# Mixer A's visits split into half steps, and the first two projection tiles interleaved

## What is computed

```python
h = rmsnorm(x, g_mix); z = h @ w_in            # 44 tiles of 128 columns
# mixer A: 16 heads x 64, ALiBi, three windows (128,1), (512,4), (2048,16), outputs mixed by their softmax denominators
# mixer B: 16 query heads, 4 key heads, window 128, with a learned sink
y = concat(oa * silu(ga), ob * silu(gb)); h = x + y @ w_out
out = h + (p @ w_ple) * sigmoid(rmsnorm(h, g_ple) @ w_pg); final rmsnorm
```

## Time and profile before

| | us |
|---|---|
| median of 3 runs | 2344.28 (2338.28 to 2345.48) |
| the profiled execution | 2341.7 |
| its span | 2339.9 |
| TensorE busy in it | 2278.0 |
| VectorE, ScalarE, POOL busy | 905.0, 565.0, 771.8 |

### The profile page before, as it was taken

How to read it: one execution, slowest core, us unless ns; L and a number is a source line. 1 busy time by engine, 2 the same in 40 slices (tenths; PEclk the granted TensorE clock), 3 DMA queues, 4 the chain that set the end, 5 groups by cost and what they waited for, 6 DMA issues and landing times.

```text
span 2339.9 us, 39175 instructions
## 1 busy us (share of the span) xinstructions
PE 2278.0 (97%) x15570; PEld 2179.3 (93%) x15570; DVE 905.0 (39%) x2334; ACT 565.0 (24%) x1562; POOL 771.8 (33%) x783
## 2 busy tenths in 40 slices
PE   4999999999999999999999999999999999999996
PEld 4999999999999999999988999899999999999996
DVE  7123333333324413455555424343233373222235
ACT  5122222222222212323544310210000030000374
POOL 2232222222222133222222233343333344555564
PEclk9999999999999999999999999999999999999998
DMA  5144454444444425455464454454343555444666
GB/s 196 61 125 96 104 117 96 108 114 96 109 111 96 107 71 147 131 147 146 138 160 142 135 174 131 158 139 111 86 102 92 122 164 133 113 115 109 194 202 224
DMA packets 542140, 299.71 MB, mean 128 GB/s; under 512 B 245140, under 2 KB 507300, under 8 KB 540668
## 3 DMA queue, kind: packets, MB, share of 16 engines
q1 hardware_dynamic: 464277, 254.82, 41.1%
q10 hardware_dynamic: 77680, 42.39, 6.3%
HBM read 230.76 MB, written 66.36 MB: 127 GB/s over the span
## 4 chain that ended last, share of the span: by engine, by line
PE 90%; DVE 4%; DMA 2%; ACT 2%; POOL 1%; issue 0%; SPq 0%; DVEq 0%; ACTq 0%; POOLq 0%
PE psum L1081 26%; PE psum L1083 26%; PE psum L1082 26%; PE psum L889 3%; PE psum L911 2%; PE psum L922 2%; PE psum L951 1%; PE psum L979 1%; PE psum L966 1%; DMA h_stage<-h_scratch 1%; DVE x_n L1554 1%; DVE act_lo L1545 1%; PE psum L986 1%; POOL w_lo L845 0%; DMA x_in<-in_x_prompt 0%; DVE act_lo L1912 0%
## 5 line engine op out<-in xcount | busy, mean ns | idle before, releaser
L1081 PE MATMUL psum<-act_hi,w_hi 128*128 128x344 f32 x4032 | 1303.4, 323 | 6.6 <-POOL w_lo L845 5.3
L1083 PE MATMUL psum<-act_hi,w_lo 128*128 128x344 f32 x4032 | 1286.9, 319 | 0.0
L1082 PE MATMUL psum<-act_lo,w_hi 128*128 128x344 f32 x4032 | 1286.1, 319 | 0.0
L1081 PEld LDWEIGHTS psum<-act_hi,w_hi 128*128 128x128 f32 x4032 | 758.2, 188 | 17.9 <-issue 12.4
L1083 PEld LDWEIGHTS psum<-act_hi,w_lo 128*128 128x128 f32 x4032 | 757.5, 188 | 0.0
L1082 PEld LDWEIGHTS psum<-act_lo,w_hi 128*128 128x128 f32 x4032 | 757.2, 188 | 0.2
L843 POOL CAST w_hi<-w_raw 128x512 fp32r<-128x512 f32 (+1 forms) x352 | 222.8, 633 | 1464.1 <-PE psum L1083 1274.9
L845 POOL TENSOR_TENSOR w_lo<-w_raw,w_hi 128x512 fp32r<-128x512 f32 (+1 forms) x390 | 508.7, 1306 | 59.6 <-ACT w_hi L1488 31.3
L1657 DVE COPY prob_t<-psum 128x512 f32<-128x512 f32 (+1 forms) x56 | 35.5, 634 | 391.5 <-PE psum L922 391.5
L1958 DVE TENSOR_TENSOR t_gate<-psum,acc 128x344 f32<-128x344 f32 x48 | 24.7, 515 | 224.9 <-PE psum L1083 224.9
L1889 DVE TENSOR_TENSOR h_row<-psum,h_row 128x344 f32<-128x344 f32 x48 | 22.1, 513 | 212.9 <-PE psum L1083 212.9
(11 more groups left out here) (208 smaller groups left out, 1787.4 us busy)
## 6 DMA issues: line engine op xcount, KB each, us to landing
w_raw<-in_w_in SPq DMA_DIRECT2D x208, 256.0 KB, 3.0
w_raw<-in_w_pg SPq DMA_DIRECT2D x94, 256.0 KB, 2.8
w_raw<-in_w_out SPq DMA_DIRECT2D x64, 256.0 KB, 2.7
z_scratch<-stage ACTq DMA_DIRECT2D x72, 172.0 KB, 1.9
h_scratch<-h_row ACTq DMA_DIRECT2D x16, 516.0 KB, 2.7
x_in<-in_x_prompt SPq DMA_DIRECT2D x8, 1024.0 KB, 5.1
zq<-z_scratch SPq DMA_DIRECT2D x32, 256.0 KB, 3.9
out<-z_sq SPq DMA_DIRECT2D x128, 64.0 KB, 2.8
```

What stands on the lines that cost most here:

```text
L1081: pe.matmul(psum[:, bank, 0:T3], hi_w, hi_a[:, k, rows], start=(k == 0), stop=False, skip_group_check=True)
L1082: pe.matmul(psum[:, bank, 0:T3], hi_w, lo_a[:, k, rows], start=False, stop=False, skip_group_check=True)
L1083: return pe.matmul(psum[:, bank, 0:T3], lo_w, hi_a[:, k, rows], start=False, stop=stop, skip_group_check=True)
```

## The change

Mixer A gets half steps: 8 in 144 positions, an even one at 36 (s // 2) with the values of chunks already turned and then the scores of one or two chunks, an odd one 22 positions behind it with only turns, of one or two chunks. A pair has 12 half steps, and pair n's last four are shared with the next pair's first four. A chunk has a slot of two banks (2 and 3, or 4 and 5) for scores and turn alike; copies go back in place into `prob`, `prob_t` is gone; the two halves of the output have banks 6 and 7. Where two chunks are scored in a visit, both wait for what the first waits for. VectorE and SP follow, with the low half of the values turned as the first thing of half step 2.

The head: three slots for x, normalised in place; `pick` loaded ahead of `g_row`; three tiles turned before the first unit; the units of the first two weight tiles interleaved (by thirds), with eight groups of weights held; in the very first unit all products with `act_hi` first, then those with `act_lo`; the other tiles turned at positions 12, 17, 26, 39, 44 and 48. The rest is a later load of the sink table and merged semaphores.

```diff
-X_FIRST = 4
-X_LATER = {4: 4, 8: 5, 13: 6, 19: 7, 27: 8}
+X_FIRST = 3
+X_LATER = {12: 3, 17: 4, 26: 5, 39: 6, 44: 7, 48: 8}
+X_BANKS = 24
+LO_AFTER = {1: (0,), 2: (1, 2), 4: (3,), 5: (4, 5), 7: (6,)}
+HEAD_TILES = 2
+HEAD_UNITS = [(i, t) for t in range(3) for i in range(HEAD_TILES)]
+HEAD_BANKS = [0, 1, 6, 7, 0, 1]
+HEAD_GROUPS = 8
...
+def x_place(u):
+
+    return 2 + u % 6 if u < X_BANKS else 2 + (u - X_BANKS) % 4
...
+def x_before(u):
+
+    return u - 5 if u < X_BANKS + 4 else u - 3
...
+def last_unit(tile):
+
+    return 2 * HEAD_TILES + tile if tile < HEAD_TILES else 3 * tile + 2
...
+def freed_before(u):
+
+    if u < 4:
+        return 0
+    return u - 3 if u < len(HEAD_UNITS) else u - 1
...
 NCH = len(A_PARTS)
-SCORE_AT = [0, 2, 3, 4, 5, 6, 8]
-TURN_AT = [7, 4, 5, 6, 8, 9, 10]
-TURN_ORDER = [1, 2, 3, 0, 4, 5, 6]
-SCALE_AT = [6, 3, 4, 5, 6, 7, 9]
-SCALE_ORDER = [1, 2, 3, 4, 0, 5, 6]
-PLACE = [(0, 8, 12, 4, 8, 12, 0), (4, 8, 12, 0, 8, 12, 4)]
-PLACE_FREE = [(-1, 3), (-1, 4), (-1, 5), (-1, 6), (0, 1), (0, 2), (0, 0)]
-A_STEPS = 13
+A_HALVES = 8
+A_STEPS = 12
+SCORE_AT = [0, 2, 2, 4, 4, 6, 8]
+SCORED_WITH = [0, 1, 1, 3, 3, 5, 0]
+TURN_AT = [7, 3, 3, 5, 5, 7, 9]
+TURN_ORDER = [1, 2, 3, 4, 0, 5, 6]
+SCALE_ORDER = [1, 2, 3, 4, 5, 0, 6]
+A_SLOT = [0, 0, 1, 0, 1, 1, 1]
+PLACE = [0, 4, 8, 4, 8, 4, 4]
+PLACE_FREE = [(-1, 0), (-1, 6), (-1, 4), (0, 1), (0, 2), (0, 3), (0, 5)]
 SQUARE_AT = [1, 2, 4, 6]
 NSQ = len(SQUARE_AT)
 V_HIGH, V_LOW, K_HIGH, K_LOW = range(NSQ)
...
+def scored_before_step(n, c):
+
+    if c == NCH - 1:
+        return scored_before(n + 1, A_FAR) if n + 1 < PAIRS else scored_before(n, c)
+    return scored_before(n, SCORED_WITH[c])
...
-    for g in range(7, WG * (NZ - 2) + 7):
-        tile, part = divmod(g - 7, WG)
-        put(16 * (3 * tile + 2) + 4 * (part + 1), "weights", g)
+    for g in range(HEAD_GROUPS + 2, WG * (NZ - 2) + 7):
+        tile, part = divmod(ring_before(g - 2), WG)
+        put(16 * last_unit(tile) + 4 * (part + 1), "weights", g)
...
-        for s in range(NCH if n + 1 < PAIRS else A_STEPS):
-            put(176 + 144 * n + (144 * s // NCH if n + 1 < PAIRS else 14 * s), "a", n, s)
+        for s in range(A_HALVES if n + 1 < PAIRS else A_STEPS):
+            put(176 + 144 * n + (36 * (s // 2) + 22 * (s % 2) if n + 1 < PAIRS else 32 * (s // 2) + 20 * (s % 2)), "a", n, s)
+        put(176 + 144 * n + 50, "a_low", n)
...
-        x_in, x_n, g_row = at(W_END, ("x_in", [P, 2, D], F32), ("x_n", [P, 2, D], F32), ("g_row", [P, D], F32))
+        x_in, x_sq, g_row, w_hi_head, w_lo_head = at(
+            W_END, ("x_in", [P, 3, D], F32), ("x_sq", [P, D], F32), ("g_row", [P, D], F32),
+            ("w_hi_head", [P, HEAD_GROUPS - WRING, WG, P], F32R), ("w_lo_head", [P, HEAD_GROUPS - WRING, WG, P], F32R))
...
             for i, (r0, n) in enumerate(ROW_TILES):
-                if i >= 2:
-                    sp.wait_ge(sem("x_normed"), i - 1)
-                sp.dma_start(x_in[0:n, i % 2, :], x_p[r0:r0 + n, :] if i < 8 else x_s).then_inc(sem(f"x_loaded{i % 2}"), 16)
+                if i >= 3:
+                    sp.wait_ge(sem("x_turned"), 4 * (i - 2))
+                sp.dma_start(x_in[0:n, i % 3, :], x_p[r0:r0 + n, :] if i < 8 else x_s).then_inc(sem(f"x_loaded{i % 3}"), 16)
                 if i == 0:
                     sp.dma_start(ident[:], a["c_ident"]).then_inc(sem("consts"), 16)
+                    sp.dma_start(pick[:], a["c_pick"]).then_inc(sem("consts"), 16)
                     sp.wait_ge(sem("x_loaded0"), 16)
                     sp.dma_start(g_row[:], bcast_rows(a["g_mix"][0:1, :], P)).then_inc(sem("consts"), 16)
-                elif i == 1:
-                    sp.dma_start(pick[:], a["c_pick"]).then_inc(sem("consts"), 16)
...
-                for g in {1: (0, 1), 2: (2,), 3: (3,), 5: (4,)}.get(i, ()):
+                for g in {2: (0, 1), 3: (2, 3), 4: (4, 5), 5: (6, 7)}.get(i, ()):
                     weights(g)
-            for g in range(5, 7):
+            for g in range(HEAD_GROUPS, HEAD_GROUPS + 2):
                 weights(g)
 
...
                     more = n + 1 < PAIRS
                     if s == 1:
                         store_squares(n, V_HIGH)
+                        load_zv(n, 0)
                         sp.wait_ge(sem("fstat_stored"), 16 * (n + 1))
                         sp.dma_start(n_stat[:, n % 2].rearrange("p m h b -> p (m h) b"), fs_dram[n % 2].rearrange("m (b p) -> p m b", p=P),
                                      allow_slow_non_contiguous=True).then_inc(sem("nstat_loaded"), 16)
...
                     elif s == 2:
-                        load_zv(n, 0)
                         load_v_nat(n, 1)
                     elif s == 3:
-                        store_squares(n, V_LOW)
-                    elif s == 4:
                         load_v_nat(n, 0)
...
-                        if more:
-                            load_zv(n + 1, 1)
                         store_squares(n, K_LOW)
                     elif s == 8 and more:
+                        load_zv(n + 1, 1)
+                    elif s == 9 and more:
                         sp.wait_ge(sem("a_biased"), 2 * scored_before(n, NCH - 1) + 2)
                         load_bias(n + 1)
                         sp.wait_ge(sem("a_scored"), 2 * scored_before(n, NCH - 1) + 2)
                         load_zq("a", n + 1, 0)
-                    for half, at_s in ((1, 9), (0, 12)):
+                    for half, at_s in ((1, 9), (0, 11)):
                         if s == at_s:
                             store_o("a", n, half)
...
+                elif e[0] == "a_low":
+                    store_squares(e[1], V_LOW)
...
             def a_scores(n, c):
-                first = scored_before(n, c)
+                first, bank = scored_before_step(n, c), 2 + 2 * A_SLOT[c]
...
-                        if i == 0 and first:
-                            pe.wait_ge(sem("a_biased"), 2 * (first - 1) + h + 1)
-                        mm = pe.matmul(psum[:, 2 + h, col:col + w], queries(half), keys(half), start=True, stop=True)
+                        if i == 0 and h == 0 and first:
+                            pe.wait_ge(sem("a_biased"), 2 * first)
+                        mm = pe.matmul(psum[:, bank + h, col:col + w], queries(half), keys(half), start=True, stop=True)
                         if i == len(pieces) - 1:
                             mm.then_inc(sem("a_scored"), 1)
 
...
                 pe.wait_ge(sem("a_copied0"), before + 1)
                 pe.wait_ge(sem("a_copied1"), before + 1)
...
-                        mm = pe.matmul(psum[HD * h:HD * h + HD, 6, c0:c1:step], values[:, HD * h:HD * h + HD], prob_t[:, h, x * P:(x + 1) * P],
+                        mm = pe.matmul(psum[HD * h:HD * h + HD, bank, c0:c1:step], values[:, HD * h:HD * h + HD], prob_of(c)[:, h, x * P:(x + 1) * P],
                                        start=(c in (1, 4) and x == 0), stop=(c in (A_FAR, NCH - 1) and x == len(pieces) - 1), skip_group_check=True)
                 mm.then_inc(sem("a_summed"), 1)
 
             def a_turns(n, c):
-                before = turned_before(n, c)
+                before, bank = turned_before(n, c), 2 + 2 * A_SLOT[c]
                 pe.wait_ge(sem("a_scaled"), scaled_by(n, c))
                 for h in range(2):
                     if before:
                         pe.wait_ge(sem(f"a_copied{h}"), before)
...
 
             def a_step(n_, s_):
                 for n, s in a_walked(n_, s_):
-                    if s in SCORE_AT:
-                        a_scores(n, SCORE_AT.index(s))
+                    for c in TURN_ORDER:
+                        if TURN_AT[c] == s - 1:
+                            a_values(n, c)
+                for n, c in a_chunks(n_, s_):
+                    a_scores(n, c)
                 for n, s in a_walked(n_, s_):
-                    if s - 1 in TURN_AT:
-                        a_values(n, TURN_AT.index(s - 1))
-                for n, s in a_walked(n_, s_):
-                    if s in TURN_AT:
-                        a_turns(n, TURN_AT.index(s))
+                    for c in TURN_ORDER:
+                        if TURN_AT[c] == s:
+                            a_turns(n, c)
 
             def b_step(n_, s_):
                 g = n_ // 2
...
                 if k % WG == 0:
                     pe.wait_ge(sem("w_split"), GROUP[what, tile, k] + 1)
 
+            def first_unit():
+
+                rows = slice(0, T3)
+                pe.wait_ge(sem("x_hi"), 4 * 3)
+                for k in range(KT):
+                    if k in X_LATER:
+                        x_turn(X_LATER[k])
+                    group_wait("in", 0, k)
+                    hi_w, lo_w = split_place(GROUP["in", 0, k - k % WG], WG)
+                    pe.matmul(psum[:, 0, 0:T3], hi_w[:, k % WG, :], act_hi[:, k, rows], start=(k == 0), stop=False, skip_group_check=True)
```

(54 more changed lines are left out.)

154 lines of the change are left out of this document (93 added, 61 removed).

## The result

The changed kernel takes 2369.24 us (median of four runs, 2366.61 to 2373.76) against 2343.89 us of the kernel before on the same chip: ratio 1.0115, 95% interval 1.009 to 1.0139. It is about 25 us **slower**. I had forecast 2340.8, within 2328 to 2352, so both the forecast and the range missed. The profiled execution is the slowest of the four, 2373.8 us with a span of 2371.9.

A forecast was written before the change was run, and what follows sets the result against it. TensorE, busy 97% of the span, was taken as the bound: only what it does or waits for counts. Mixer A's visits -12.5, copy wait +17 and head -8 gave -3.5 us: 2340.8 by the median, range 2328 to 2352.

The forecast's parts named there:

- Visits, -12.5 us: Mixer A: four visits of values and scores lose 0.55 us each, turns 0.01; -12.5 us over eight pairs (-17 to -4).
- Alone it would have given the wrong sign: Rival for the whole kernel: counting drains only, mixer A only gains, giving the first rival's time, 2323.8; no chance given.
- Wait inside a visit of turns, +17: Mixer A, half steps 3, 5, 7: second chunk waits for the first's copies, 0.71 us 24 times, +17 (+9 to +24).
- The chain between scores and turns: Mixer A: two chunks are biased, exponentiated and scaled within 22 positions, 10.3 us; effect 0.
- Two us spare: 0: Mixer A: chunk 1 ready at 8.1 us (needed 10.3), chunk 2 at 9.4 (needed 11.7), so no cost.
- It eats half a us of the spare: Mixer A: turning the low square ends about 10 us after half step 1 began; chunk 1's scores are out at 9.6.
- 2 us or more to spare: SP's queue: zv, v_nat, bias and zq are issued a few positions earlier or later, each with that margin.
- The second rival: Mixer A: low values load late behind SP's stores, turns start 1.5 us late in each pair; +12, 2352.8; chance 0.17.
- Head, -8: First projections: last row tile turned and TensorE at position 48 at 66.7 us, before 74.8; -8 us (-14 to -3).
- The sum: Whole kernel: -12.5 + 17 - 8 = -3.5 us, 2338.2, by the median 2340.8; no change.

The follow-up runs named there:

- e8: Changed kernel with e5's four edits, and the low half of v_nat loaded by its own event at position 58 (52 in the last pair): 2326.05 us, ratio 0.9921.
- e1: Changed kernel without the wait on the previous chunk's copies inside a_turns: 2359.33 us, ratio 1.007.
- e2: Changed kernel with own buffers for the low half of the values and its square, loaded with the high half: 2348.63 us, ratio 1.0021.
- e3: Changed kernel with the edits of e1 and e2 together: 2337.86 us, ratio 0.9972.
- e4: Changed kernel with every odd half step at position 26 instead of 22, except in the last pair: 2360.91 us, ratio 1.008.
- e5: Changed kernel with e3's edits, the last row tile's turn at position 56, and half step 3 at 26 (24 in the last pair): 2343.88 us, ratio 1.0002.

## Why the prediction was wrong

- **Visits, -12.5 us: right.** In e8, where no visit waits, they sum to 158.1 us (12.3 + 24.6 + 121.2 for all others) against 168.8 before: -10.7. A visit of turns of one chunk costs 0.87 us for a stream of 0.85, so turns are free to enter and leave. A visit of values and scores loses 0.60 us (that of half step 4 costs 3.59 for streams of 2.99, by the prediction's 0.053 us for 128 columns) where I took 0.55. (Visits that score the far chunk lose 1.1 us more, in both kernels.) So the rule of the Trainium skill, "TensorEngine Tiling (Array Packing)", Key Properties, that a change of the tiling mode drains the engine, agrees with these visits (0.60 us lost where the mode changes, 0.02 where it doesn't). Alone it would have given the wrong sign for the kernel.
- **Wait inside a visit of turns, +17: right in mechanism and price.** A visit takes 2.20 us with it and 1.53 without, 16 times, which is 10 to 11 us; in half step 3, the other eight times, a longer wait covered it.
- **The chain between scores and turns, put at 0: this step failed.** The prediction found "Two us spare: 0", and of the low half's load that "It eats half a us of the spare". The working gave 9.0 us from half step 1 to the low half's landing; it was 12.6 in pair 2. Term by term: VectorE's square of the high half was done at 3.1, not 2.3. SP was 2.0 us late for it, since at the same visit it has the previous pair's two biases, zq and output to issue, behind four weight groups; of bias and zq I wrote that they have "2 us or more to spare", and asked when they would be late, not whom they make late. The stores took 3.8 us to issue, not 2.2. The load took 3.6, less than the 4.5 assumed. Behind that the chain itself was 1.7 us longer than in the earlier trace rows (bias to scaled 10.4 us, not 8.7), all of it in the scaling. Some 3.4 us late and 1.7 longer, against 2.2 spare, is a wait of 2.9 us; TensorE's idle time is recorded as 2.58.
- **The second rival had the mechanism, not the size.** It named that wait at +12 us, from one duration (6.5 us for the load) that never occurred: the loads of the low half took 3.3 to 4.5 us in the eight pairs. The lateness came from the queue ahead of the load. And the rival priced idle time only: 16.8 us of waits for the scaling made half step 3 24.6 us dearer, with another 3 us or so of projections at half clock behind them.
- **Head, -8: the mechanism right, the size off.** The changed kernel's profile shows -3.5, the head alone -5.4 by the medians. TensorE reached position 48 at 68.8 us, not 66.7, VectorE being 1.9 late with the last tile (65.85 against 64), and then lost some 2.6 us more to the half clock, for which the sum had no term.
- **The sum.** In the profiled executions mixer A's +33.2 is -10.7 for the clean visits, +10.7 for the copy waits of half steps 5 and 7, and some 33 for half step 3 over its clean 12.3 with the slow projections behind it. Of these 33 about 5 are the hidden copy waits. By the medians the whole change is +25.4, where the two profiled executions are 32.1 apart; how the 6.7 us less are shared out isn't known. e1 and e2 measured the two main losses as 9.9 and 20.6, and some 6 us more are the second chunk's late scaling that e2 and e3 still have and e8 doesn't.

## What to carry to other kernels

When steps are merged, work out for each DMA the time at which its queue comes to it, with everything that now stands ahead at the same visit; a landing time from an unhurried queue doesn't tell when a load is there. Take away all waits of a place together, or expect the next one (the load, then the stores, then the second chunk, then v_nat). And price a stall of TensorE with the half clock that can come behind it: in the head it made 5 us of 2.

## What the runs showed of the hardware

- **Half clock after a short stall, but not after every one.** Idle 2.58 us ahead of the turns brought the granted clock to the lower level for the visit and 3 us more, in pairs 2 and 4 of the changed kernel. The length of the stall doesn't decide alone. In the changed kernel 1.92 us ahead of the turns cost just themselves in pair 1 (4.39 us for the visit) and were followed by 2.7 us of slow projections in pair 6 (5.08). Stalls of 0.59 and 0.74 us (e2, e4) had nothing behind them. In e5 six idle times of 1.0 to 1.95 us ahead of half step 4 cost just themselves (4.66 to 5.60 us for the visit, 3.59 clean), and two of 1.97 and 2.16 us cost 7.25 and 7.45. Two of these by TensorE's timeline, pair 3 and pair 1:

```profile
436.31 1.75 PE L987 MATMUL psum<-prob,v_nat 128*64 128x128 f32 x28 [1.95 <-issue]
255.67 2.10 PE L987 MATMUL psum<-prob,v_nat 128*64 128x128 f32 x28 [1.97 <-issue]
```

- **VectorE stands while GpSimd splits weights.** The row of VectorE at 343.52 above is an instruction on 2 elements in each partition that took 1.14 us, 0.16 elsewhere; the next row takes 2.11 us for two pieces in place of 0.61. GpSimd's timeline of the changed kernel at that time:

```profile
343.35 1.29 POOL L918 TENSOR_TENSOR w_lo<-w_raw,w_hi 128x512 fp32r<-128x512 f32 x1
...
345.27 1.26 POOL L918 TENSOR_TENSOR w_lo<-w_raw,w_hi 128x512 fp32r<-128x512 f32 x1
```

The first ends at 344.64, VectorE's at 344.66; the second ends at 346.53, VectorE's two pieces at 346.69. By the Trainium skill, "SBUF — State Buffer", Who interferes with whom, the two engines share a pair of ports, a VectorE instruction with two inputs in SBUF contends for it with a GpSimd instruction that reads SBUF, and the one that issues second is blocked until the other's instruction ends; the first of these pairs of rows agrees (VectorE's has two inputs, and began 0.17 us behind GpSimd's). The second chunk's late scaling in e2 looks the same: there a multiplication on 2 elements ends at 341.49 and GpSimd's subtraction at 341.47. So does a row of the kernel before, inside the 3.76 us that I took from the earlier trace rows: one VectorE instruction of 1.15 us from 436.92 on, where GpSimd subtracts until 438.05. Scaling chunk 1 took 2.4 us in e2, where nothing fell on it. No run here took the splits away, so how much of the 1.7 us they explain wasn't measured.
